# Decoder layer on one core: gate-2 sums dealt over the up iterations, four adaLN pieces in the attention, and other waits for the down units

## The reference

```python
mod = silu(c) @ w_ada + b_ada               # 1024 x 6144: six vectors of 1024
sh1, sc1, g1, sh2, sc2, g2 = split(mod, 6)
hn   = modulate(rmsnorm(h), sh1, sc1)
proj = hn @ w_in                            # u, q, k, v, qi, ki, wi
y_ssm, y_attn = s5_mixer(u, ...), dsa_mixer(q, k, v, qi, ki, wi)
h = h + g1 * (concat(rmsnorm(y_ssm), rmsnorm(y_attn)) @ w_out)
hn2 = modulate(rmsnorm(h), sh2, sc2)
up = causal_dwconv(hn2 @ w_up)              # width 3, 2 x 2816 columns
h = h + g2 * ((gelu(gate) * val) @ w_down)  # 2816 x 1024
```

## Time and profile before

| | |
|---|---|
| three runs, median (lowest to highest) | 836.96 us (835.87 to 839.49) |
| profiled execution: own time, span | 839.14 us, 837.3 us |
| mean granted TensorE clock of the span | 0.929 |
| TensorE busy | 716.7 us, 86% |
| VectorE busy | 488.5 us, 58% |
| ScalarE busy | 330.3 us, 39% |
| GpSimd busy | 257.9 us, 31% |
| a unit's low part on GpSimd (L460), x35 | 4.62 us each |
| a unit's high part on ScalarE (L652), x26 | 1.91 us each |
| HBM traffic over the span | 109 GB/s |

### The profile page before, as it was taken

One profiled execution on the slowest core, in us unless ns is written; L12 is line 12 of the kernel. 1 busy time (PEld: TensorE's weight loads), 2 busy tenths in 40 slices (PEclk: granted clock), 3 DMA queues, 4 the chain that ended last, 5 costly groups with the idle time before them and its releaser, 6 DMA issues.

```text
span 837.3 us, 9955 instructions
## 1 busy us (share of the span) xinstructions
PE 716.7 (86%) x3524; PEld 571.3 (68%) x3524; DVE 488.5 (58%) x870; ACT 330.3 (39%) x478; POOL 257.9 (31%) x204
## 2 busy tenths in 40 slices
PE   0689999997759579889595999999999995999968
PEld 0667876775546346678495688888888874888856
DVE  3989597996799766679559455554444543000004
ACT  4154444446213532623465355454555442111100
POOL 1007697029004000002024133444433342444320
PEclk9999999997778859899797899999999997999979
DMA  9932311250055591065541133222333321122202
GB/s 339 313 101 76 102 50 51 101 151 0 1 57 58 171 397 60 0 255 198 167 160 51 51 100 100 84 80 87 100 100 100 100 100 50 63 89 100 101 4 97
DMA packets 65606, 91.44 MB, mean 109 GB/s; under 512 B 11914, under 2 KB 39330, under 8 KB 65443
## 3 DMA queue, kind: packets, MB, share of 16 engines
q1 hardware_dynamic: 60800, 84.72, 31.9%
q10 hardware_dynamic: 4771, 6.26, 2.4%
HBM read 86.28 MB, written 4.69 MB: 109 GB/s over the span
## 4 chain that ended last, share of the span: by engine, by line
issue 42%; PE 26%; DVE 15%; POOL 9%; ACT 3%; DMA 3%; POOLq 1%; SPq 0%; ACTq 0%; DVEq 0%
POOL w_lo L460 9%; PE bank L1530 6%; PE bank L1532 6%; PE bank L1531 6%; PE bank L1535 2%; DVE arena L1097 2%; PE bank L1843 1%; DMA arena<-in_w_ada 1%; PE bank L1756 1%; DVE w_lo L1091 1%; DVE arena L1243 1%; PE bank L1736 1%; DVE stat L1240 1%; DMA xh<-in_x 1%; DMA y_dram<-xh 1%
## 5 line engine op out<-in xcount | busy, mean ns | idle before, releaser
L460 POOL TENSOR_TENSOR w_lo<-w_raw,w_hi 128x2048 fp32r<-128x2048 f32 x35 | 161.7, 4622 | 435.6 <-ACT w_hi L652 218.9
L1530 PE MATMUL bank<-act_hi,w_hi 128*128 128x512 f32 (+2 forms) x384 | 148.1, 386 | 5.0 <-DVE act_lo L1473 5.0
L1531 PE MATMUL bank<-act_lo,w_hi 128*128 128x512 f32 (+2 forms) x384 | 146.7, 382 | 0.0
L1532 PE MATMUL bank<-act_hi,w_lo 128*128 128x512 f32 (+2 forms) x384 | 146.5, 382 | 0.0
L1530 PE MATMUL bank<-w_hi,act_hi 128*128 128x512 f32 x240 | 101.1, 421 | 5.9 <-DVE act_lo L1132 4.3
L1532 PE MATMUL bank<-w_hi,act_lo 128*128 128x512 f32 x240 | 97.0, 404 | 0.0
L1531 PE MATMUL bank<-w_lo,act_hi 128*128 128x512 f32 x240 | 97.0, 404 | 0.0
L652 ACT ACTIVATE w_hi<-w_raw 128x2048 fp32r<-128x2048 f32 x26 | 49.8, 1914 | 110.5 <-PE bank L1532 96.1
L1530 PEld LDWEIGHTS bank<-act_hi,w_hi 128*128 128x128 f32 x384 | 73.2, 191 | 20.0 <-issue 6.1
L1530 PE MATMUL bank<-w_hi,ff_hi 128*128 128x512 f32 x176 | 71.7, 408 | 16.7 <-DVE arena L1512 10.1
L1490 DVE SCALAR_TENSOR_TENSOR conv<-bank,vec_cols,conv 128x511 f32<-128x511 f32 x44 | 33.0, 749 | 87.1 <-ACT conv L1001 86.8
(11 more groups left out here) (295 smaller groups left out, 1183.4 us busy)
## 6 DMA issues: line engine op xcount, KB each, us to landing
w_raw<-in_w_up SPq DMA_DIRECT2D x44, 512.0 KB, 4.7
w_raw<-in_w_down SPq DMA_DIRECT2D x22, 512.0 KB, 3.9
w_raw<-in_w_in SPq DMA_DIRECT2D x10, 1024.0 KB, 5.1
arena<-in_w_ada SPq DMA_DIRECT2D x10, 1024.0 KB, 8.4
arena<-in_w_ada SPq DMA_DIRECT2D x4, 2048.0 KB, 18.5
xh<-in_x SPq DMA_DIRECT2D x8, 512.0 KB, 9.3
w_raw<-in_w_out SPq DMA_DIRECT2D x4, 1024.0 KB, 12.2
arena<-in_w_ada ACTq DMA_DIRECT2D x2, 2048.0 KB, 11.2
```

What stands on the lines that cost most here:

```text
L460: nc.gpsimd.tensor_tensor(w_lo[:, slot, 0:width], w_raw[:, slot, 0:width], w_hi[:, slot, 0:width].bitcast(F32), ALU.subtract).then_inc(S[" ...
L1530: T.matmul(dst, lhs_hi, rhs_hi, start=start, stop=False)
L1531: T.matmul(dst, lhs_hi, rhs_lo, start=False, stop=False)
L1532: return T.matmul(dst, lhs_lo, rhs_hi, start=False, stop=stop)
```

## The change

- **Gate 2.** The 16 steps of pieces 6 and 7 leave the place ahead of VectorE's up loop and are dealt singly behind the taps of banks 0, 1 and 2 in iterations 1 to 5, and bank 0 of iteration 6. VectorE's loop is written out for iterations 0 to 7, then comes the gate-2 row, then a loop over 8 to 10. TensorE's gate-2 matmuls stand between iterations 7 and 8.
- **Down.** Unit n (1 to 9) waits for the `ff_lo` tiles that it reads itself instead of for all 22; the last unit alone is run bank by bank, with 6 matmuls a bank instead of 12, and units 9 and 10 no longer wait together for the last low part.
- **Attention.** The 24 steps of three pieces from i = 22 become 32 steps of four, four at each i from 24 to 31. Piece 0 is loaded in two halves as soon as the S5 products have read that memory (`y_mm` 2 and 4), ahead of the load of `y_ssm`; the order of SyncE's later loads changes. Behind the attention two pieces are left, not three, and the last stands behind the low part of the last `w_out` unit.
- **Second norm.** VectorE scales tiles 0 and 2 (L1469 of the changed kernel), ScalarE only tile 1 before tile 3; the partition sums of pieces 2 to 5 stand ahead of tile 3 of units 2 and 3.

```diff
-ADA_STEPS = {22: 2, 23: 2, 24: 2, 25: 2, 26: 3, 27: 3, 28: 3, 29: 3, 30: 2, 31: 2}
+ADA_STEPS = {n: 4 for n in range(24, 32)}
+GATE2_AT = {(1, 0): 1, (1, 1): 1, (1, 2): 1, (2, 0): 1, (2, 1): 1, (2, 2): 1, (3, 0): 1, (3, 1): 1, (3, 2): 1,
+            (4, 0): 1, (4, 1): 1, (4, 2): 1, (5, 0): 1, (5, 1): 1, (5, 2): 1, (6, 0): 1}
+GATE2_SUM = 8
@@
+            sp.wait_ge(S["y_mm"], 2)
+            later_ada(0, (0,))
+            sp.wait_ge(S["y_mm"], 4)
+            later_ada(0, (1,))
             sp.wait_ge(S["y_stored"], 16)
             load(y_ssm, y_dram.rearrange("(a p) n -> p a n", p=P), "y_loaded")
-            later_ada(0)
+            later_ada(1)
             load(gate1_row, b_ada[0, 2048:3072].partition_broadcast(P), "gate1_row")
+            out_unit(1)
+            sp.wait_ge(S["ada_used"], 1)
+            later_ada(2)
+            sp.wait_ge(S["ada_used"], 2)
+            later_ada(3)
             for t in range(TT):
                 load(xh[:, t, :], x[0, t * P:(t + 1) * P, :], "x_again")
-            later_ada(1)
-            out_unit(1)
             out_unit(2)
-            sp.wait_ge(S["ada_used"], 1)
-            later_ada(2)
+            sp.wait_ge(S["y_attn_ready"], TT)
+            later_ada(4)
+            later_ada(5)
             out_unit(3)
@@
             rstd_of_h((0, 1, 2))
+            for t in (0, 2):
+                signal(V.tensor_scalar(hn[:, t, :], xh[:, t, :], rstd_h[:, t:t + 1], None, ALU.mult), "hn_even")
             mixed(1, 3)
@@
+                    for _ in range(steps.get(q, 0)):
+                        n, k = 6 + gate2_at[0] // KD, gate2_at[0] % KD
+                        late_ada(n, k, k + 1)
@@
+            with pe.Fori(1, GATE2_SUM) as j:
+                up(j)
             pe.wait_ge(S["ada_used"], 8)
             for i in range(2):
                 ins = T.matmul(bank[6 + i][:], ones[:], gate2_acc[i], start=True, stop=True)
             ins.then_inc(S["ada_sum_ready"], 1)
-            with pe.Fori(1, UPS) as j:
+            with pe.Fori(GATE2_SUM, UPS) as j:
                 up(j)
@@
-            pe.wait_ge(S["ff_lo_ready"], FT)
-            for n in range(1, FT // 2 - 2):
+            for n in range(1, FT // 2 - 1):
+                pe.wait_ge(S["ff_lo_ready"], 2 * n + 2)
                 pe.wait_ge(S["lo_ready"], U_DOWN + n + 1)
                 down(slot(U_DOWN + n), 2 * n, False)
+            pe.wait_ge(S["ff_lo_ready"], FT)
             pe.wait_ge(S["lo_ready"], UNITS)
@@
-                    for k in range(FT - 4, FT):
-                        wh, wl = down_weights(slot(UNITS - 2 + (k - FT + 4) // 2))
+                    for k in (FT - 2, FT - 1):
+                        wh, wl = down_weights(slot(UNITS - 1))
```

More of the change, by code:

```diff
@@ L1481, in _, with convolved @@
                 hn_lo(k, slice(3 * P, SEQ), KD + k)
-            late_ada(6)
-            late_ada(7)
-            with dve.Fori(0, UPS) as j:
+            gate2_at = [0]
+            def convolved(j, steps):
                 for q in range(4):
@@ L1938, in _ @@
                 for t in range(TT):
-                    out_product(n, t)
-                if n >= 2:
-                    pe.wait_ge(S["ada_used"], 2 * n)
-                    pe.wait_ge(S["h_ready"], 1)
-                    for i in (2 * n - 4, 2 * n - 3):
-                        ins = over_partitions(bank[4][:, 4 * i:4 * i + 4], ada_late_acc[2 + i])
-            ins.then_inc(S["ada_sum_ready"], 1)
+                    if n >= 2 and t == TT - 1:
+                        pe.wait_ge(S["ada_used"], 2 * n)
+                        pe.wait_ge(S["h_ready"], 1)
+                        for i in (2 * n - 4, 2 * n - 3):
+                            ins = over_partitions(bank[4][:, 4 * i:4 * i + 4], ada_late_acc[2 + i])
+                        if n == 3:
+                            ins.then_inc(S["ada_sum_ready"], 1)
+                    out_product(n, t)
             def turn_hn(k):
```

36 lines of the change are left out of this document (18 added, 18 removed).

## The result

| | before | after |
|---|---|---|
| median (lowest to highest) | 836.41 us (833.30 to 839.49) | 800.16 us (799.62 to 801.28) |
| profiled execution: time, span | 839.14, 837.3 us | 801.28, 799.5 us |
| ratio of the times, 95% interval | | 0.957 (0.953 to 0.961) |

The forecast was 802.2 us, range 798.0 to 808.5. In the profiled executions the span is 37.8 us shorter, where the sum said 34.8; the medians of all runs are 836.41 - 800.16 = 36.3 us apart. The profiled execution of the kernel before was 2.7 us above its median, that of the changed kernel 1.1 above its own.

What follows compares the result with a forecast made beforehand. TensorE, 86% busy, was taken as the bound, with gains only in its idle joints. Terms 10.3 + 12.0 + 9.3 + 0.7 + 2.5 = 34.8 us off 836.96 gave 802.2 us, range 798 to 808.5.

Steps and rivals of the forecast that it cites:

- start of up, with the matmuls by ones: TensorE's gap ahead of up iteration 1: starts 12.4 us earlier, less 2.1 for two matmuls; 10.3 us gained.
- start of down: TensorE's wait for the gate-2 row ahead of the down units goes, with the low clock behind it; 12.0 us gained.
- last down units: Wait for the last low part ahead of units 9 and 10 goes, with its low clock; 9.3 us gained.
- since the idle time is much nearer to none: Start of up: reason for taking 10.3 us, without a clock fall in about 2 us of idle time, from 8.4 to 10.3.
- Steps within the up iterations: Three steps an iteration add 2.3 us to VectorE's work in a 22.3 us period, under cover, and cost nothing.
- Second norm: Between residuals and first modulation: the last residual ends earlier, giving 0.7 us of gain (-1 to 2).
- the last residual's end at 409.4: Second norm: tile 2's residual at 402.9, then square, root and VectorE's two scalings lead to this time, against 410.10.
- Attention: Attention up to the output norm: 3.8 us less through earlier logits, minus 1.3 for the store; 2.5 us gained.
- The delayed store: Attention: piece 0's early second half delays the S5 output's store by 0 to 4.3 us, taken as 1.3.
- the sum would be 0.5 us lower: Attention: if engines alternate queues by packet, a store with few large packets loses under 1 us, changing the sum thus.
- the clock case: Up to the end: TensorE's long run without rest lowers its clock, making the kernel slower than before; chance 0.02.
- The better case: Attention and second norm: no delay of the store and 1 us at the norm, giving 799.5 us; chance 0.08.

Runs made afterwards that it cites:

- E2: Changed kernel with the sixteen steps of the last two pieces put back ahead of VectorE's up loop; 809.79 us, ratio to the kernel before 0.968.
- E1: Changed kernel with VectorE adding the gate-2 row behind its last up iteration again; 810.19 us, ratio to the kernel before 0.967.
- E3: Changed kernel with both waits of the down units as in the kernel before; 810.02 us, ratio to the kernel before 0.966.
- E4: Changed kernel with the attention part undone: step table, SyncE's loads and three pieces behind the attention as before; 806.63 us, ratio 0.964.
- E5: Changed kernel with the second-norm part undone: ScalarE scales tiles 0 to 2, partition sums behind the products; 798.97 us, ratio 0.953.
- E8: Changed kernel with ScalarE's three DMA issues for gate 2 moved ahead of its squares of the second half; 793.37 us, ratio 0.945.
- E9: Changed kernel with four of its 32 attention steps moved to i = 22 and 23, loads unchanged; 804.27 us, ratio 0.961.
- E10: Kernel before with its 24 attention steps dealt as three at each i from 24 to 31, nothing else; 830.14 us, ratio 0.993.
- E6: Changed kernel with the second half of piece 0 loaded behind `y_ssm` instead of ahead of it; 800.09 us, ratio 0.955.
- E7: Changed kernel with the last 48 of 96 small matmuls of the first up iteration ordered bank by bank; 799.92 us, ratio 0.955.

## Why the prediction was right, and where its sizes were off

Measured terms are distances between before and after in the table and in the timelines: 7.6 us are gained up to the modulation; 18.8 up to iteration 1; the first tap of iteration 10 comes 681.80 - 278.14 = 403.66 and 665.35 - 278.07 = 387.28 us behind the store, 16.4 gained; the last matmul of down unit 8 stands at 801.29 and 772.85, 28.4 gained; 37.7 at the end.

| term | predicted | measured |
|---|---|---|
| attention and second norm | 2.5 + 0.7 | 7.6 (6.0 attention, -1.1 second norm, 2.7 clock) |
| start of up, with the matmuls by ones | 10.3 (8.4 to 10.3) | 18.8 - 7.6 - 2.4 = 8.8 |
| start of down | 12.0 | 28.4 - 16.4 = 12.0 |
| last down units | 9.3 | 37.7 - 28.4 = 9.3 |
| sum | 34.8 | 37.7 |

- **Start of up.** Right in its mechanism (E2). The gap closed by 18.8 - 7.6 = 11.2 us against 12.4: the idle time left is 1.6 us where the prediction said about 2, but the clock fell in it, which the prediction had at the lower end of its range (1.9 us; measured 3.41 - 1.86 = 1.55). Choosing the upper end "since the idle time is much nearer to none" was the mis-sized step. The matmuls by ones cost 1.7 instead of 2.1; the other 0.6 or so of the 2.4 in the table is the period of 22.40 instead of 22.31.
- **Steps within the up iterations.** Right: 0. One step in each of iterations 2 to 6 met GpSimd's operation and took 1.95 us instead of 0.74, under cover. Of VectorE, and GpSimd's operation that ends at 487.40:

```profile
485.33 0.75 DVE L1499 SCALAR_TENSOR_TENSOR conv<-bank,vec_cols,conv 128x510 f32<-128x510 f32 x1
486.00 1.95 DVE L1116 SCALAR_TENSOR_TENSOR arena<-arena,c_col 128x512 f32<-128x512 f32 x1
```
```profile
482.77 4.63 POOL L466 TENSOR_TENSOR w_lo<-w_raw,w_hi 128x2048 fp32r<-128x2048 f32 x1 [5.78 <-ACT w_hi L996]
```

  The step ends 0.55 us behind GpSimd's end, the tap, which reads PSUM, took its usual 0.75 meanwhile. The Trainium skill ("SBUF — State Buffer", Who interferes with whom) has the two exclude each other for the whole instruction; the trace agrees.
- **Start of down, last down units.** Right to 0.1 us, and E1 and E3 give 12.0 and 8.3 when each is undone alone.
- **Second norm.** The sign of the term was wrong. Between first and last residual 31.2 us became 30.2, and 0.25 us more went ahead of the modulation: 1.3 in all, which looks like the 0.7 of the prediction but comes from the one piece less. The part itself costs 1.1 us (before against E4) to 1.4 (E5 against after), and undone alone it is worth nothing at the end (E5). The step that failed is the chain that ends in "the last residual's end at 409.4": what moved the residuals up is that VectorE's last piece no longer stands in front of them (before, to 401.2), and that belongs to the attention part; the second-norm part's two scalings only put 1.3 us ahead of the last residual. One more reason was wrong: the add of tile 0 met GpSimd's low part (3.70 instead of 0.69 us). The last piece had that collision before; the prediction said that the piece would lose it, and not that the residual would get it. That the row's issue holds up the modulation was right, and E8 turned it into 4.6 us.
- **Attention.** The mis-sized term: 6.0 us (E4) instead of 2.5. The direction and the mechanism (the steps ahead of the top-k and the low parts go, the first `w_glu` product starts earlier) held in E9 and E10. At the logits of i = 26 the prediction had 3.4 us of gain and 6.4 came: the second low part ended 302.00 + 1.29 = 303.29 instead of 307.57, 4.3 us earlier with the store's delay in, 1.0 more than the 4.6 - 1.3 of the prediction; and the product with its bias row took from 303.39 to 308.75, 5.4 us, instead of 7.4 (from 307.67 to 315.06), since its bias row and first five matmuls ran at the full clock and before nothing of it did. Against E4 3.6 us are left of the gain at the first residual. The other part is behind the attention: one piece less on VectorE is worth 2.3 us there (E4), which the prediction had at nothing, as it took TensorE for the bound.
- **What the clock did.** 6.0 - 1.1 is not 7.6. E4 reached its first residual 2.7 us ahead of the kernel before, with the same instructions up to there: about half at the `w_glu` product and half at the attention's end, where the clock was low for longer before (first line, 65.9 to 71.9 us behind the store) than in E4 (second line, the same distance).

```profile
344.00:350.00 6.00, 6.00 (x19) 4.29 (x20) 3.82 (x17) 0.51 (x1) 0.00 (x0) 0.52 0.00 1
```
```profile
341.28:347.28 6.00, 4.87 (x20) 3.02 (x19) 4.16 (x14) 1.27 (x2) 0.00 (x0) 0.78 0.00 0
```

  These 2.7 us are a difference between two executions, not shown to be a gain of the change. Without them the terms sum to 35.0. So the closeness of the total has luck in it: 1.5 us too much at the start of up stand against 4.9 - 3.2 = 1.7 too little in attention and second norm.
- **The delayed store.** 1.0 us (E6) where the prediction took 1.3. The Trainium skill ("DMA: Bandwidth & Descriptors", Queues, rings and completion order) has a DMA engine take turns between queues by packets, from which the prediction worked out a delay under 1 us; the measured one is at that edge. A shorter delay would make the gain larger and the time lower, so "the sum would be 0.5 us lower" has the sign of the time. E10 reaches the modulation as early as the changed kernel without any early load, so no gain from the load shows.
- **Rivals.** None came true. TensorE ran 346 us, from 449.07 to 795.56, at a granted clock of 1.00, so the clock case is out. The better case, 799.5 us, is within 0.7 us of the measured time, but its own parts (1.3 for the store, 0.3 for the second norm) give 800.6, and neither came: the store was delayed, and the gain lay in the attention.

## What to carry to other kernels

Work that an engine does ahead of a loop in one block can be dealt over the loop's iterations wherever it has slack, even single instructions that a neighbour holds up; what has to be watched is not their sum but whom each instruction stands in front of: two steps between two low parts cost 3 us, half of it by the clock (E9), a DMA issue of 3.8 us and two shorter ones ahead of a modulation 4.6 (E8). When a wait goes, look for the next one before sizing the gain: at the start of up a low part of GpSimd stood 0.35 us under the wait for the bank, and an edit that removed the latter alone was worth nothing (E7). A clock that falls in a short wait is part of the price, and it makes the same instructions differ by some 1 to 3 us from one execution to the next, so parts are better compared by distances in a trace than by the total.
